# A delta-rule mixer's pair products issued ahead of its token transposes, with retention's reciprocals in halves, the slab splits and the gate's product placed beside the levels of the triangular inverse

## The chip, the cores and the metric

One core of a Trainium2 chip runs the whole program. The metric is the device time in microseconds (us) of one execution, as the median of several runs.

## The reference, cut to what matters

The program computes two blocks of a network on 512 tokens of width 1024, in float32. The change touches only the first block, whose two layers each run three mixers side by side: a delta-rule mixer of four heads of 64 (`rwkv7_mixer`), a retention mixer (`retention_mixer`) and latent attention (`mla_mixer`). Their outputs are joined and multiplied by `w_out`.

```python
def rwkv7_mixer(p, mu, w0, w2, a0, a2, g2, k_k, k_a, r_k, gn_w, gn_b, v_first, v_res):
    ...
    g = jax.nn.sigmoid(gd) @ g2
    ...
    def step(state, inp):
        rt, kt, vt, wt, kkt, at = inp
        sa = jnp.einsum('bhvk,bhk->bhv', state, -kkt)
        state = (state * wt[:, :, None, :] + sa[..., None] * (kkt * at)[:, :, None, :]
                 + vt[..., None] * kt[:, :, None, :])
        return state, jnp.einsum('bhvk,bhk->bhv', state, rt)
    ...
    bonus = jnp.sum(r_h * k_h * r_k, axis=-1, keepdims=True) * v_h
    y = (y + bonus.reshape(B, S, RW_DIM)) * g
    return y, v_first

def retention_mixer(p, positions):
    ...
    y = y * lax.rsqrt(jnp.mean(y * y, axis=-1, keepdims=True) + NORM_EPS)
    return jax.nn.silu(g) * y.reshape(B, S, RET_DIM)
```

The scan over tokens is computed in chunks of 64. Within a chunk the recurrence is a lower triangular system, and its inverse is needed.

## The kernel before, in words

Every tensor stays on the chip: `h` is the residual stream, `arena` is a pool of 53 tiles of 128x512 float32 (`A(t)` is tile t), `con` holds constants, and `banks` are the eight PSUM banks. Weights come as slabs of up to 128x2048 through a ring of two slots. A slab is split into a high and a low part for exact products of reduced-precision matmuls (L580 to L582): ScalarE casts the high part (`prepare`, L1222), VectorE subtracts it for the low part (`prepare`, L1689), and only then may SyncE load the next slab into the slot (L2466).

Each engine has its own program, written by hand, and runs it in order. TensorE's groups take the banks in turn: `group` waits until the bank's occupant of eight groups before was released by the engine that owns it, which counts up `act_released` (ScalarE) or `dve_released` (VectorE). `taken(key)` is that release, `finished(key)` is the end of the group's matmuls. `psum_ready` is counted up at the end of a group.

The place of the change is the function `rwkv(l)` on TensorE and what answers to it on ScalarE, VectorE and GpSimd (POOL). In order, in each of the two layers:

1. `retention` ends with the sums of squares "rss" (L606), whose root ScalarE takes (`deviation`, L1208). VectorE inverts it (`invert`, L1652, a reciprocal of a whole tile), multiplies it into the output (L2000) and that by the gate (L2002). The second L2002 counts up `mix_ret_ready`.
2. VectorE's `decayed` makes the scaled keys; its last instructions (L1978) free TensorE through `scan_inputs_ready`. Before that TensorE has put "bonus" into two banks, which VectorE reads at L2007.
3. TensorE transposes four tensors to token-major form, two groups each ("tok", eight groups of four transposes, L789), and ScalarE copies them out (L1385).
4. `gram` makes three sets of pair products of 64x64 blocks, "L", "N" and "M", two banks each, 32 matmuls a set (L808). ScalarE copies L (L1202). VectorE masks N and L into the first inverse Xt and X (L2020, L2022), adds the identity (L2025, L2026, the latter counting up `inverse_ready`) and masks M (L2030).
5. `low_rank(l, 2, ...)` is the gate's product "z" (two matmuls of 64x512, L606), copied by ScalarE into tiles 39 and 40 after a wait for `mix_ret_ready`, since retention's output lies there.
6. The inverse goes through five levels (block sizes 2 to 32). In a level `blocks` (L820) makes T1 for both heads of a pair, ScalarE copies T1 (L1202), then `blocks` makes Xt and X for both, each of 16 matmuls of 64x64, and VectorE adds them (L2038). GpSimd masks the next level's factor (L2431). The last level has no X. Behind levels 0 and 1 stands a group MV (`by_token`, L834).
7. `by_token` makes W and U (L834), then come the chunk products (L881), the chain of states (L930) and the outputs (L943), the two norm sums and the output projection (L580).

```python
                gram("L", "act", Af, Bf)
                gram("N", "dve", Bf, Af)
                gram("M", "dve", Kf, Af)
                low_rank(l, 2, slice(64, 128))
                last = len(LEVELS) - 1
                for n in range(len(LEVELS)):
                    for e in range(2):
                        pe.wait_ge(lower_off_ready, cnt.next(lower_off_ready))
                        if n:
                            pe.wait_ge(*taken(("Xt", l, n - 1, e)))
                        else:
                            pe.wait_ge(inverse_ready, cnt.next(inverse_ready))
                        blocks(("T1", l, n, e), "act", 19 + e, 23 + e)
```

## Time and profile before

| | us |
|---|---|
| median of 3 runs | 2264.26 |
| lowest and highest | 2262.85 and 2276.31 |
| the profiled execution | 2263.33 |
| its span, first to last instruction | 2261.5 |
| TensorE busy in the span | 2066.6 (91%) |
| VectorE busy | 1254.9 (55%) |
| ScalarE busy | 812.9 (36%) |
| GpSimd busy | 88.6 (4%) |
| mean granted TensorE clock | 0.956 of full speed |

The profile's page gives totals. A change of order in one stage is read from the timeline and the chain of waits of that stage: about 276 to 326 us in the first layer and 1019 to 1069 us in the second. A float32 matmul appears as two records, so a group of 16 matmuls of 64x64 is 32 records. A granted clock of 1.00 is 2.4 GHz and 0.50 is 1.2 GHz. Since each engine runs in order, an instruction can be late because of what stands ahead of it on its own engine, and TensorE can wait on a bank as well as on data.

### The profile page before, as it was taken

What the parts mean: (1) busy time and instruction counts of PE and PEld (TensorE: products, weight loads), DVE (VectorE), ACT (ScalarE), POOL (GpSimd) and SP (SyncE); (2) the same over time, 40 slices, a digit from 0 to 9 for tenths busy, and PEclk for the clock granted to TensorE, in tenths of its full rate; (3) what the DMA queues carried; (4) which work ended last, traced back from release to release, by engine and by line L of the source; (5) the groups of instructions that cost most, each with busy time, mean ns of one, the idle gap of its engine ahead of it and who ended that gap; (6) DMA issues with size and microseconds to landing.
All of it is one profiled execution on the core that took longest, in us unless ns stands there. A gap on an engine that the chain in (4) does not pass through costs nothing.

```text
span 2261.5 us, 29485 instructions
## 1 busy us (share of the span) xinstructions
PE 2066.6 (91%) x12698; PEld 1672.7 (74%) x12698; DVE 1254.9 (55%) x1579; ACT 812.9 (36%) x1075; POOL 88.6 (4%) x61
## 2 busy tenths in 40 slices
PE   6998688999999999868899999999999987899776
PEld 5786476888888887637688888887777666697664
DVE  8474756643444636566554334467766634563764
ACT  3244433322222324443332222246454533262522
POOL 4010020000000001012000000000000000100000
PEclk9999799999999999988999999999999989899788
DMA  5220011222322322001023233133222222121010
GB/s 196 103 77 1 1 41 38 94 96 83 112 104 77 107 101 77 1 1 40 20 93 103 80 109 108 65 122 121 77 91 92 76 75 93 33 100 64 1 38 37
DMA packets 25472, 166.81 MB, mean 74 GB/s; under 512 B 2816, under 2 KB 3072, under 8 KB 9472
## 3 DMA queue, kind: packets, MB, share of 16 engines
q1 hardware_dynamic: 25344, 164.93, 20.8%
q8 instruction: 101, 1.65, 0.3%
q14 instruction: 27, 0.22, 0.0%
HBM read 162.82 MB, written 2.10 MB: 73 GB/s over the span
## 4 chain that ended last, share of the span: by engine, by line
PE 77%; DVE 13%; ACT 7%; issue 3%; DMA 0%; DVEq 0%; SPq 0%; ACTq 0%
PE bank L580 21%; PE bank L581 21%; PE bank L582 21%; PE bank L606 4%; PE bank L820 2%; DVE ring_low L1689 2%; DVE arena L1652 2%; PE bank L727 2%; ACT ring_high L1222 1%; PE bank L714 1%; DVE arena L2171 1%; ACT arena L1481 1%; PE bank L1154 1%; DVE arena L1990 1%; PE bank L808 1%
## 5 line engine op out<-in xcount | busy, mean ns | idle before, releaser
L580 PE MATMUL bank<-arena_split,ring_high 128*128 128x512 f32 x2252 | 895.7, 398 | 63.0 <-DVE ring_low L1689 42.8
L581 PE MATMUL bank<-arena_split,ring_high 128*128 128x512 f32 x2252 | 884.2, 393 | 0.0
L582 PE MATMUL bank<-arena_split,ring_low 128*128 128x512 f32 x2252 | 883.4, 392 | 0.0
L580 PEld LDWEIGHTS bank<-arena_split,ring_high 128*128 128x128 f32 x2252 | 427.7, 190 | 167.5 <-DVE ring_low L1689 37.5
L581 PEld LDWEIGHTS bank<-arena_split,ring_high 128*128 128x128 f32 x2252 | 428.0, 190 | 92.5 <-issue 4.6
L582 PEld LDWEIGHTS bank<-arena_split,ring_low 128*128 128x128 f32 x2252 | 427.4, 190 | 90.2
L1689 DVE TENSOR_TENSOR ring_low<-ring,ring_high 128x2048 fp32r<-128x2048 f32 (+3 forms) x161 | 344.6, 2142 | 148.9 <-ACT ring_high L1222 147.9
L1222 ACT ACTIVATE ring_high<-ring 128x2048 fp32r<-128x2048 f32 (+3 forms) x161 | 284.3, 1769 | 388.5 <-PE bank L582 387.3
L1240 ACT ACTIVATE arena<-bank 128x512 f32<-128x512 f32 x72 | 43.1, 599 | 268.1 <-DVE bank L1670 268.0
L1202 ACT ACTIVATE arena<-bank 128x512 f32<-128x512 f32 (+3 forms) x113 | 58.6, 533 | 177.4 <-PE bank L582 98.0
L2118 DVE TENSOR_TENSOR arena<-arena,bank 128x512 f32<-128x512 f32 x44 | 30.3, 688 | 119.7 <-PE bank L582 118.1
L1670 DVE TENSOR_TENSOR bank<-bank,rstd 128x512 f32<-128x512 f32 x72 | 50.2, 697 | 77.5 <-PE bank L582 77.5
L1696 DVE TENSOR_TENSOR arena_split<-arena,arena_split 128x512 fp32r<-128x512 f32 x94 | 61.5, 688 | 52.8 <-ACT arena_split L1228 52.7
L1652 DVE RECIPROCAL arena<-arena 128x512 f32<-128x512 f32 x23 | 77.0, 3348 | 23.4 <-ACT arena L1208 23.3
L606 PE MATMUL bank<-arena 128*128 128x512 f32 (+8 forms) x256 | 87.6, 495 | 0.6 <-issue 0.6
L606 PE MATMUL bank<-arena,con 128*128 128x512 f32 (+1 forms) x122 | 61.6, 630 | 11.5 <-DVE arena L1645 4.3
L1228 ACT ACTIVATE arena_split<-arena 128x512 fp32r<-128x512 f32 x94 | 54.6, 622 | 28.7 <-DVE arena L2092 20.8
L580 PE MATMUL bank<-ring_high,arena_split 128*128 128x256 f32 (+1 forms) x208 | 61.4, 295 | 0.0
L582 PE MATMUL bank<-ring_high,arena_split 128*128 128x256 f32 (+1 forms) x208 | 60.5, 291 | 0.0
L581 PE MATMUL bank<-ring_low,arena_split 128*128 128x256 f32 (+1 forms) x208 | 60.5, 291 | 0.0
L1664 DVE TENSOR_TENSOR arena<-bank,rstd 128x512 f32<-128x512 f32 (+1 forms) x43 | 29.4, 688 | 53.2 <-PE bank L582 53.0
L820 PE MATMUL bank<-arena 64*64 64x64 f32 x1792 | 55.8, 221 | 3.3 <-issue 3.2
(285 smaller groups left out, 1897.3 us busy)
## 6 DMA issues: line engine op xcount, KB each, us to landing
ring<-slabs_in SPq DMA_DIRECT2D x122, 1024.0 KB, 4.8
ring<-slabs_in SPq DMA_DIRECT2D x32, 704.0 KB, 4.1
con<-con_in SPq DMA_DIRECT2D x1, 2176.0 KB, 9.7
h<-x_in SPq DMA_DIRECT2D x4, 512.0 KB, 7.4
out<-h SPq DMA_DIRECT2D x4, 512.0 KB, 2.6
ring<-slabs_in SPq DMA_DIRECT2D x3, 512.0 KB, 3.7
ring<-slabs_in SPq DMA_DIRECT2D x2, 768.0 KB, 4.3
arena<-gates_in SPq DMA_DIRECT2D x1, 1536.0 KB, 8.8
```

What stands on the lines that cost most here:

```text
L580: pe.matmul(out, weight[0], right[0], start=start, stop=False)
L581: pe.matmul(out, weight[0], right[1], start=False, stop=False)
L582: return pe.matmul(out, weight[1], right[0], start=False, stop=stop)
L606: mm = pe.matmul(b[out_rows, 0:N], w, r, start=(k == 0), stop=(k == len(weights) - 1))
L820: mm = pe.matmul(bk[rows_of(s), block(hp, j)], A(left)[at], A(right)[at], start=(hp == 0 and j == 0), stop=(hp == 1 and j == NT - 1))
L1202: f(dst, b[rows, 0:n], func, scale=scale).then_inc(cnt.up(act_released), 1)
L1222: f(ring_high[:, n % SLOTS, 0:cols], ring[:, at % SLOTS, 0:cols], ACT.Copy).then_inc(cnt.up(slab_high_ready), 1)
L1228: f(R(dst), src, ACT.Copy).then_inc(cnt.up(high_ready), 1)
L1652: dve.reciprocal(A(t)[:, 0, :], A(t)[:, 0, :]).then_inc(cnt.up(dve_done), 1)
L1670: tt(b[:, :], b[:, :], rstd[:, :], MUL).then_inc(cnt.up(scaled_ready), 1)
L1689: tt(ring_low[:, n % SLOTS, 0:cols], ring[:, at, 0:cols], ring_high[:, n % SLOTS, 0:cols].bitcast(F32), SUB).then_inc(cnt.up(slab_split), 1)
L1696: tt(R(dst), src, R(high).bitcast(F32), SUB).then_inc(cnt.up(parts_ready), 1)
```

## The change

On TensorE the three `gram` calls stand ahead of the transposes (the helper functions move with them, unchanged), and the gate's product stands behind level 3. ScalarE copies L first, then the transposes; it casts the two slabs of the output projection one behind level 2 and one behind the last level, and copies z behind level 3's T1. VectorE no longer inverts and multiplies retention's factor ahead of the bonus: it does the bonus, multiplies retention's sum by its gate, and works off the rest between the additions of the levels, the reciprocal in four halves of 256 columns. No other stage is touched. GpSimd's and SyncE's programs are the same.

```diff
 # TensorE
                 pe.wait_ge(scan_inputs_ready, cnt.next(scan_inputs_ready))
...
+                gram("L", "act", Af, Bf)
+                gram("N", "dve", Bf, Af)
+                gram("M", "dve", Kf, Af)
                 pe.wait_ge(values_ready, cnt.next(values_ready))
                 for n, src in enumerate((14, 33, 35, 27)):
...
-                gram("L", "act", Af, Bf)
-                gram("N", "dve", Bf, Af)
-                gram("M", "dve", Kf, Af)
-                low_rank(l, 2, slice(64, 128))
                 last = len(LEVELS) - 1
                 for n in range(len(LEVELS)):
...
+                    if n == last - 1:
+                        low_rank(l, 2, slice(64, 128))
 # ScalarE
                 for hp in range(2):
                     deviation(("rss", l, hp), A(hp)[:, 0, :], 64)
-                prepare(f"out{l}_0")
-
+                for e in range(2):
+                    copy_out(("L", l, e), A(17 + e)[:, 0, :])
                 for n in range(4):
...
-                for e in range(2):
-                    copy_out(("L", l, e), A(17 + e)[:, 0, :])
-
-                act.wait_ge(mix_ret_ready, cnt.next(mix_ret_ready))
-                for i in range(2):
-                    copy_out(("z", l, 2, i), A(39 + i)[:, 0, :])
                 for n in range(len(LEVELS)):
                     for e in range(2):
                         copy_out(("T1", l, n, e), A(49 + e)[:, 0, :])
                     if n < 2:
                         copy_out(("MV", l, n), A(35 + n)[:, 0, :])
+                    if n == 2:
+                        prepare(f"out{l}_0", 1)
+                    if n == len(LEVELS) - 2:
+                        act.wait_ge(mix_ret_ready, cnt.next(mix_ret_ready))
+                        for i in range(2):
+                            copy_out(("z", l, 2, i), A(39 + i)[:, 0, :])
+                prepare(f"out{l}_0")
 # VectorE
                 decayed()
-                for hp in range(2):
-                    invert(("rss", l, hp), hp)
-                    y = A(39 + hp)[:, 0, :]
-                    tt(y, y, A(hp)[:, 0, :], MUL).then_inc(cnt.up(dve_done), 1)
-                    dve.wait_ge(cnt.sem, cnt.value)
-                    tt(A(2 + hp)[:, 0, :], y, A(23 + hp)[:, 0, :], MUL).then_inc(cnt.up(mix_ret_ready if hp else dve_done), 1)
                 dve.wait_ge(values_ready, cnt.next(values_ready))
                 for hp in range(2):
                     dve.wait_ge(psum_ready, finished(("bonus", l, hp)))
                     b = bank(("bonus", l, hp))
                     tt(A(37 + hp)[:, 0, :], b[:, :], v_(hp), MUL).then_inc(cnt.up(dve_released), 1)
-                prepare(f"out{l}_0")
+                for hp in range(2):
+                    dve.wait_ge(*taken(("ry", l, hp)))
+                    tt(A(39 + hp)[:, 0, :], A(39 + hp)[:, 0, :], A(23 + hp)[:, 0, :], MUL).then_inc(cnt.up(dve_done), 1)
+                dve.wait_ge(cnt.sem, cnt.value)
+
+                def retention_factor(hp, half):
+
+                    dve.wait_ge(*taken(("rss", l, hp)))
+                    r = A(hp)[:, 0, half * (T // 2):(half + 1) * (T // 2)]
+                    dve.reciprocal(r, r).then_inc(cnt.up(dve_done), 1)
+
+                def retention_output(hp):
+
+                    dve.wait_ge(cnt.sem, cnt.value)
+                    tt(A(2 + hp)[:, 0, :], A(39 + hp)[:, 0, :], A(hp)[:, 0, :], MUL).then_inc(cnt.up(mix_ret_ready if hp else dve_done), 1)
+
+                beside = {(0, 0): lambda: retention_factor(0, 0), (0, 1): lambda: retention_factor(0, 1),
+                          (1, 0): lambda: retention_factor(1, 0), (1, 1): lambda: retention_factor(1, 1),
+                          (2, 0): lambda: retention_output(0), (2, 1): lambda: retention_output(1),
+                          (3, 0): lambda: prepare(f"out{l}_0", 1)}
...
                             tt(M[:, e, :], M[:, e, :], b[:, :], ADD).then_inc(cnt.up(dve_released), 1)
+                        if (n, e) in beside:
+                            beside[n, e]()
+                prepare(f"out{l}_0")
                 state = flat(14, 3)
```

TensorE's order around the inverse in the kernel before, from retention's sums of squares (L606 with `con`) to the last level. L789 are the transposes, L808 the three grams, L606 with `small` the gate's product, L820 the levels' blocks, L834 MV, then W and U.

```order
L606 MATMUL bank<-arena,con 128x512 x4
L789 MATMUL bank<-con,arena 128x128 x32
L808 MATMUL bank<-arena 64x64 x96
L606 MATMUL bank<-arena,small 128x512 x2
L820 MATMUL bank<-arena 64x64 x96
L834 MATMUL bank<-arena 64x64 x16
...
L820 MATMUL bank<-arena 64x64 x256
L834 MATMUL bank<-arena 64x64 x64
```

The same stretch in the changed kernel, where the grams are L798, the transposes L838, the levels' blocks L810 and MV, W and U L824.

```order
L606 MATMUL bank<-arena,con 128x512 x4
L798 MATMUL bank<-arena 64x64 x96
L838 MATMUL bank<-con,arena 128x128 x32
L810 MATMUL bank<-arena 64x64 x96
L824 MATMUL bank<-arena 64x64 x16
...
L810 MATMUL bank<-arena 64x64 x192
L606 MATMUL bank<-arena,small 128x512 x2
L810 MATMUL bank<-arena 64x64 x64
L824 MATMUL bank<-arena 64x64 x64
```

The grams and the transposes change places, and the gate's product goes from ahead of level 0 to between levels 3 and 4.

VectorE's order in the kernel before, from the last instructions of `decayed` (L1978) to the additions of the levels (L2038).

```order
L1978 TENSOR_TENSOR arena<-arena,decay_end 128x512 x2
L1652 RECIPROCAL arena<-arena 128x512
L2000 TENSOR_TENSOR arena<-arena 128x512
L2002 TENSOR_TENSOR arena<-arena 128x512
L1652 RECIPROCAL arena<-arena 128x512
...
L2007 TENSOR_TENSOR arena<-bank,arena 128x512 x2
L1689 TENSOR_TENSOR ring_low<-ring,ring_high 128x2048 x2
L2020 TENSOR_TENSOR arena<-bank,con 128x512
...
L2030 TENSOR_TENSOR arena<-bank,con 128x512 x2
L2038 TENSOR_TENSOR arena<-arena,bank 128x512 x18
```

The same stretch in the changed kernel, where L1980 ends `decayed`, L2003 is the bonus, L2006 the product with the gate, L2013 a half reciprocal, L2018 retention's output, L1691 a slab's low part and L2053 the levels' additions.

```order
L1980 TENSOR_TENSOR arena<-arena,decay_end 128x512 x2
L2003 TENSOR_TENSOR arena<-bank,arena 128x512 x2
L2006 TENSOR_TENSOR arena<-arena 128x512 x2
L2035 TENSOR_TENSOR arena<-bank,con 128x512
...
L2045 TENSOR_TENSOR arena<-bank,con 128x512 x2
L2053 TENSOR_TENSOR arena<-arena,bank 128x512 x2
L2013 RECIPROCAL arena<-arena 128x256
...
L2018 TENSOR_TENSOR arena<-arena 128x512
...
L1691 TENSOR_TENSOR ring_low<-ring,ring_high 128x2048
L2053 TENSOR_TENSOR arena<-arena,bank 128x512 x4
L1691 TENSOR_TENSOR ring_low<-ring,ring_high 128x2048
```

The bonus stands directly behind `decayed`, nothing long stands between it and the masks, and the reciprocals and slab splits are spread among the additions.

## Rows read from the trace of the kernel before

**Rows 1.** The page, engines' busy us, share of the span and instructions.
```profile
PE 2066.6 (91%) x12698; PEld 1672.7 (74%) x12698; DVE 1254.9 (55%) x1579; ACT 812.9 (36%) x1075; POOL 88.6 (4%) x61
```

**Rows 2.** Chain of waits, first layer, 276 to 326 us: start, length, engine, tile, line.
```profile
276.05 3.27 DVE arena L1652
...
285.39 0.69 DVE arena L2007
286.22 1.94 PE bank L789 x8
288.16 4.72 PE bank L808 x192
292.88 1.91 PE bank L606 x4
294.79 1.46 issue
296.25 1.15 PE bank L820 x32
...
303.97 5.60 PE bank L820 x192
309.57 0.93 PE bank L834 x32
```

**Rows 3.** Timeline, first layer: start, length, engine, line, tiles, count, idle before and releaser.
```profile
271.36 3.70 ACT L1222 ACTIVATE ring_high<-ring 128x2048 fp32r<-128x2048 f32 x2
...
276.10 5.38 PE L789 MATMUL bank<-con,arena 128*128 128x128 f32 x24 [3.65 <-DVE arena L1978]
...
291.85 0.69 DVE L2020 TENSOR_TENSOR arena<-bank,con 128x512 f32<-128x512 f32 x1 [0.78 <-PE bank L808]
292.46 1.16 DVE L2022 TENSOR_TENSOR arena<-arena,con 128x512 f32<-128x512 f32 x1
...
297.27 1.28 DVE L2030 TENSOR_TENSOR arena<-bank,con 128x512 f32<-128x512 f32 x2
...
302.82 1.15 PE L834 MATMUL bank<-arena 64*64 64x64 f32 x32
...
353.55 0.80 PE L580 MATMUL bank<-arena_split,ring_high 128*128 128x512 f32 x1
```

**Rows 4.** Timeline, second layer, the same columns.
```profile
1018.95 4.51 PE L789 MATMUL bank<-con,arena 128*128 128x128 f32 x24 [3.65 <-DVE arena L1978]
...
1029.06 1.94 PE L789 MATMUL bank<-con,arena 128*128 128x128 f32 x8 [5.61 <-DVE arena L2007]
...
1038.35 7.62 PE L820 MATMUL bank<-arena 64*64 64x64 f32 x192 [1.29 <-issue]
...
1045.78 1.11 PE L834 MATMUL bank<-arena 64*64 64x64 f32 x32
...
1099.17 0.79 PE L580 MATMUL bank<-arena_split,ring_high 128*128 128x512 f32 x1
```

**Rows 5.** Groups of instructions, 276 to 330 us: busy us, mean ns, idle before.
```profile
L2038 DVE TENSOR_TENSOR arena<-arena,bank 128x512 f32<-128x512 f32 x18 | 12.4, 689 | 15.3 <-PE bank L820 15.3
L2431 POOL TENSOR_TENSOR arena<-arena,con 128x512 f32<-128x512 f32 x10 | 10.8, 1094 | 33.6 <-PE bank L820 17.5 <-ACT arena L1202 16.0
L1202 ACT ACTIVATE arena<-bank 128x512 f32<-128x512 f32 x16 | 9.5, 598 | 26.0 <-PE bank L820 12.8 <-PE bank L834 8.8 <-PE bank L606 3.0
L1652 DVE RECIPROCAL arena<-arena 128x512 f32<-128x512 f32 x2 | 6.7, 3342 | 0.0
L1689 DVE TENSOR_TENSOR ring_low<-ring,ring_high 128x2048 fp32r<-128x2048 f32 x2 | 4.5, 2282 | 0.0
```

**Rows 6.** Busy time in stretches: PE, PEld, DVE, ACT, POOL (records), PEclk, DMA share, GB/s.
```profile
278.00:280.00 2.00, 2.00 (x12) 2.00 (x11) 1.97 (x2) 1.38 (x3) 0.00 (x0) 0.50 0.00 0
...
290.00:292.00 2.00, 2.00 (x86) 2.00 (x81) 1.22 (x2) 1.09 (x2) 1.11 (x2) 0.50 0.88 328
298.00:300.00 2.00, 2.00 (x76) 2.00 (x73) 0.98 (x2) 0.65 (x2) 1.67 (x2) 1.00 0.04 8
1022.00:1024.00 2.00, 1.45 (x11) 1.21 (x9) 1.93 (x4) 1.74 (x4) 0.00 (x0) 0.88 0.00 0
1040.00:1042.00 2.00, 2.00 (x43) 2.00 (x42) 0.65 (x2) 0.57 (x2) 1.06 (x2) 0.50 0.00 0
```

20 lines of the change are left out of this document (10 added, 10 removed).

## The prediction, made before the changed kernel was run

> **What bounds the kernel now.** I read the page first, then the chain of waits in the two stretches that the diff touches, then the timeline there, the groups of instructions, and last the busy time with the clock. The page says that TensorE is busy for 2066.6 of 2261.5 us [rows 1], so what can be won lies in TensorE's waits and in its slow stretches, and both are in stages like this one.
>
> The chain of the first layer shows the stage. TensorE starts its transposes at 276.10, when VectorE has finished `decayed` (L1978), does 24 of 32 (six groups) in 5.38 us [rows 3], and then stops. The seventh group takes the bank of the first "bonus", and VectorE releases that bank only at L2007, at 285.39, because two whole reciprocals and four products stand ahead of it [rows 2]. The last two groups run from 286.22. Grams follow for 4.72 us and the gate's product for 1.91, then comes a gap of 1.46 in which TensorE waits for `inverse_ready`, and level 0 starts at 296.25 [rows 2]. VectorE has to mask and add eight times before it gives that signal, and again its queue sets it: it begins with L2020 at 291.85 and is at M (L2030) at 297.27 [rows 3]. From `scan_inputs_ready` to the first T1 the first layer thus takes 296.25 - 276.10 = 20.15 us. In the second layer it is 1038.35 - 1018.95 = 19.40 us, with a wait of 5.61 on the same L2007 and a gap of 1.29 before level 0 [rows 4].
>
> Within the levels TensorE is the bound. A level without MV is six groups, 192 records, in 5.60 us, and MV adds 0.93 [rows 2], with no idle time in it. VectorE's four additions of 0.69 fill less than half of that; over the stretch they come with 15.3 us of waiting for TensorE [rows 5]. Level 0 alone is slow: from its start to MV it takes 302.82 - 296.25 = 6.57 us in the first layer [rows 2, 3] and 1045.78 - 1038.35 = 7.43 in the second [rows 4], since the second T1 waits for the second `inverse_ready`, and in the second layer also because the granted clock is 0.50 from 1040 to 1042 [rows 6].
>
> **The grams first.** At 276.10 the grams start. At that point TensorE has idled for 3.65 us [rows 3] and the clock is at 0.50 [rows 6], so I take their length from the first layer, where the clock was at 0.50 too (290 to 292 [rows 6]): 4.72 us [rows 2]. Then eight groups of transposes. At 0.50 one group is 4 x 5.38 / 24 = 0.90 us [rows 3]; in the row with the clock at 0.88, 11 took 1.45 us, so a group is 0.53 [rows 6]. The grams need two banks each and the transposes the same eight, so: transposes 1 and 2 wait for the bonus, which VectorE now reads right after `decayed`, by about +1.3 us; 3 and 4 for L, copied by ScalarE; 5 and 6 for N; 7 and 8 for M. VectorE can mask N from 291.85 - 288.16 = 3.7 us after the start of the grams and has released the second M bank at 297.27 + 1.28 - 288.16 = 10.4 us after it [rows 2, 3]. What VectorE does between (two bonus products, two with the gate, 0.69 each [rows 5]) ends at +2.8, before N is there, and costs nothing. The eighth transpose group therefore starts no earlier than +10.4 and ends at +10.9 to +11.3; TensorE's own work alone would end at 4.72 + 8 x 0.53 = 9.0 to 4.72 + 8 x 0.90 = 11.9. I take +11.2 for the first T1, the bank bound with the last group at a middle length. `inverse_ready` is given before M and so is no wait any more. The gain is 20.15 - 11.2 = 8.95 us in the first layer and 19.40 - 11.2 = 8.2 in the second.
>
> **Level 0 without its wait.** It should take the six groups' 5.60: gains of 6.57 - 5.60 = 0.97 and 7.43 - 5.60 = 1.83.
>
> **The gate's product.** It costs 1.91 us [rows 2] and goes from ahead of level 0 to between levels 3 and 4, where TensorE has no gap: minus 1.91 in each layer. It is no loss against before, only the part of the 20.15 that is paid elsewhere.
>
> **VectorE's work beside the levels.** The half reciprocal has no row. A whole one is 3.34 [rows 5]; half of that is 1.67 if time goes by columns, and 3.34 if it did not. I take 1.67, since the products beside it do go by columns in the same profile (0.69 for 512, 2.28 for 2048 [rows 5]). Count from the end of Xt of the first head: X is added by +1.7, the half reciprocal ends at +3.4, the second Xt is added at +4.1, and T1 of the second head in the next level wants that at 5 x 0.93 = +4.7 with MV between. It fits with 0.6 to spare. X is added at +4.7 and the second half ends at +6.4, while TensorE's next Xt ends at +6.5. Levels 1 and 2 go alike, and retention's products (0.69) are short. In level 3 the slab's low part of 2.28 stands between: Xt of the second head is added at 1.7 + 2.28 + 0.7 = +4.6 counted as above (the end of the first Xt), and T1 of the second head wants it at 4 x 0.93 + 1.91 = +5.6, because the gate's product stands in between. Cover 1.0; without that product the wait would be 0.9. The last slab's low part falls into W and U (four groups, 3.7 us) with nothing behind it that is wanted sooner. Cost of all of it: 0, with bounds of 0 and, by the longer reciprocal, of 4 x 3.34 + 8 x 0.69 = 18.9 us on VectorE in levels 0 and 1, against 2 x (5.60 + 0.93) = 13.1 us of TensorE: 5.8 us a layer, 11.6 in all.
>
> **ScalarE and SyncE.** Two casts of 1.85 (3.70 for the pair [rows 3]) move into ScalarE's idle time, which is 26.0 us around its 16 copies [rows 5]; the one behind level 2 ends before T1 of level 3 is there. GpSimd has the same ten masks of 1.09 [rows 5], each wanted four groups after its release. The next slabs are fetched some 20 us later than now, and the output projection, which starts at 353.55 [rows 3], works on the two already split. Nothing.
>
> The Trainium skill speaks against one edit. Its page "SBUF — State Buffer", section "Who interferes with whom", says that a VectorE instruction with both inputs in SBUF competes with a GpSimd instruction that reads SBUF, one holding off the other for a whole instruction. The trace agrees in size: L2022 took 1.16 us, beside a mask on GpSimd, where its like takes 0.69 [rows 3, 5]. By that rule the slab's low part could start up to 1.09 later, which would use up the cover of 1.0; the sum would be worse by 0.1 a layer.
>
> **The sum.** 8.95 + 8.2 + 0.97 + 1.83 - 2 x 1.91 = 16.1 us. The profiled execution took 2263.33, so it would take 2247.2. It lies 0.93 under the median of 2264.26, so the median should be 2248.2.
>
> **Rivals.**
> A, VectorE's work does not fit between the additions: the half reciprocal is nearer to a whole one or the additions slip. For it speaks the slack of only 0.6 us, against it the 15.3 us of idle time [rows 5]. At the full 5.8 a layer the gain is 16.1 - 11.6 = 4.5 and the time 2259.8; at half of that, 2254.
>
> B, the clock stays at 0.50 through all transposes: T1 starts at +11.9, and one low stretch of 2 us as in 1040 to 1042, where 43 records started in place of 76 [rows 6], costs 0.9 more. That is 1.6 a layer, gain 12.9, time 2251.4.
>
> C, the clock gives back more. From MV to the projection the first layer takes 353.55 - 302.82 = 50.7 us, the second 1099.17 - 1045.78 = 53.4 [rows 3, 4]. Should the shift in time let the second layer keep its clock, 2.7 more are won: 2245.5. It can as well go the other way in the first.
>
> D, slower than before: the levels run at 1.2 GHz. They have 960 records a layer. At 2.0 / 43 against 2.0 / 76 us each [rows 6] a record costs 20.2 ns more, 19.4 us a layer and 38.8 in all: 16.1 less that is a loss of 22.7, and the time 2287.0. It decides from 16.1 / 0.0202 = 797 records at low clock, some 37 us. For it speaks that the second layer's clock fell although TensorE was nearly always busy; against it that it was 1.00 with TensorE fully busy at 298 [rows 6], and that the gaps go away. The Trainium skill's page "TensorE: Matmul & The Clock Gate", section "A second HAM failure mode: psum-queue depth-cycling", has a kernel whose small gaps between groups that cycle through the banks kept its clock switching; that is this rival, and only 1040 to 1042 bears it out here.
>
> E, the change does not do what it says: TensorE is held by the next thing, the masks of M, for much longer. Were only the gap of 4.7 to 5.6 won, the time would be 2254; the work that leaves VectorE's queue ahead of the masks, two reciprocals and two slab parts, 11.2 us [rows 5], speaks against it.
>
> **How the numbers follow.** The forecast, with a range of its own from 2244.5 to 2252, gets 0.62; A 0.13; B 0.09; C 0.08; E 0.05; D 0.03. The range of 8 in 10 goes from 2243.5 to 2256: it takes in B, C and E, half of A, and leaves out D and the far end of A. A measurement of this kernel can tell about 1%, 22.6 us, from no change. All but D and a far tail of C lie within it: faster by over 1% 0.04, within 1% 0.93, slower by over 1% 0.03.
>
> **What would show it.** Right: the first T1 about 11 us after `decayed` in both layers, no wait of TensorE on the bonus, level 0 in 5.6 us, half reciprocals of 1.7 us, the gate's product between levels 3 and 4 with no wait behind it, and everything from W on the same, only about 8 us earlier a layer. Wrong: waits of TensorE for L2053 in levels 0 to 4, a half reciprocal over 2.3 us, the clock at 0.50 inside the levels, or a T1 later than +12.

## The result and the profile after

The changed kernel takes 2251.44 us (median of 20 runs, 2244.39 to 2266.94) beside 2263.56 for the kernel before in the same comparison (20 runs, 2257.71 to 2276.31). The ratio is 0.9943 with a 95% interval of 0.9928 to 0.9959, a gain of about 13 us (9 to 16). The profiled execution took 2248.42 us with a span of 2246.6, against 2263.33 and 2261.5. The forecast was 2248.2 with a range from 2243.5 to 2256. The first row of the page answers to [rows 1]; TensorE's busy time fell by 11.2 us although its instructions are the same in number.

```profile
PE 2055.4 (91%) x12698; PEld 1662.6 (74%) x12698; DVE 1253.7 (56%) x1583; ACT 811.8 (36%) x1075; POOL 91.3 (4%) x61
```

In what follows a layer is cut at three marks: the end of VectorE's `decayed`, where TensorE begins again after 3.65 us of idling; the first T1 of level 0; and the first instruction of W. The time from the first to the third is called the stage. All of the change lies in it, but for the last slab split and the fetches of the next slabs, which now fall behind W. The marks are starts of rows of TensorE's timeline, as in [rows 3] and [rows 4].

| us | before, layer 1 | after, layer 1 | before, layer 2 | after, layer 2 |
|---|---|---|---|---|
| start to first T1 | 20.15 | 10.50 | 19.40 | 11.69 |
| first T1 to MV | 6.57 | 6.32 | 7.43 | 6.47 |
| MV to W | 23.51 | 25.57 | 23.64 | 25.68 |
| stage | 50.23 | 42.39 | 50.47 | 43.84 |
| W to the output projection | 27.22 | 29.14 | 29.75 | 29.86 |

The stage gives 7.84 + 6.63 = 14.5 us. What is left of the difference of the spans comes from parts in which TensorE's order has no edit: W to the projection is 1.9 + 0.1 longer, the stretch between the layers 2.2 longer (667.63 for 665.40), what lies ahead of the first stage 0.3 shorter, and all behind the second projection 4.4 shorter (1157.93 for 1162.33). The sum is 14.9. These outer parts jump from kernel to kernel, some of them between a few values, as the experiments show, so only the stage is evidence for a cause.

TensorE's timeline of the changed kernel in the first layer, with start, length, engine, line, tiles, count, and idle time before with its releaser:

```profile
275.81 3.03 PE L798 MATMUL bank<-arena 64*64 64x64 f32 x192 [3.65 <-DVE arena L1980]
278.77 2.84 PE L838 MATMUL bank<-con,arena 128*128 128x128 f32 x24
284.44 1.94 PE L838 MATMUL bank<-con,arena 128*128 128x128 f32 x8 [2.83 <-DVE arena L2045]
286.31 6.48 PE L810 MATMUL bank<-arena 64*64 64x64 f32 x192
292.63 1.10 PE L824 MATMUL bank<-arena 64*64 64x64 f32 x32
...
318.20 3.95 PE L824 MATMUL bank<-arena 64*64 64x64 f32 x128 [0.91 <-DVE arena L2053]
```

The same view in the second layer:

```profile
1014.97 4.50 PE L798 MATMUL bank<-arena 64*64 64x64 f32 x192 [3.65 <-DVE arena L1980]
...
1024.93 1.80 PE L838 MATMUL bank<-con,arena 128*128 128x128 f32 x8 [2.13 <-DVE arena L2045]
1026.66 6.64 PE L810 MATMUL bank<-arena 64*64 64x64 f32 x192
```

The wait on the bonus (4.74 and 5.61 before) and the wait ahead of level 0 (1.46 and 1.29) are gone. There is one in their place, again on a bank: the last two groups of transposes take M's two banks, and TensorE stands for 2.83 and 2.13 us until VectorE's mask L2045 has read them. (In the second layer there is also a stop of 0.55 us ahead of the first transposes, whose row names no releaser.) VectorE's timeline shows why it comes when it comes:

```profile
278.19 0.69 DVE L2035 TENSOR_TENSOR arena<-bank,con 128x512 f32<-128x512 f32 x1
...
283.61 1.28 DVE L2045 TENSOR_TENSOR arena<-bank,con 128x512 f32<-128x512 f32 x2
290.04 0.69 DVE L2053 TENSOR_TENSOR arena<-arena,bank 128x512 f32<-128x512 f32 x1 [5.15 <-PE bank L810]
...
291.58 1.75 DVE L2013 RECIPROCAL arena<-arena 128x256 f32<-128x256 f32 x1
```

From the first mask of N (L2035) to the end of M's (L2045) VectorE works for 6.7 us without a gap. Then it idles for 5.15, which is to say that its work is short enough but stands in an order that leaves M for last. The chain that ended last (start, length, what) gives the lengths without overlap, of level 0 in its first row and of level 1 in its last:

```profile
286.38 6.41 PE bank L810 x192
...
293.72 5.60 PE bank L810 x192
```

The busy time of stretches, with the columns of [rows 6], shows the clock on both sides of the new wait:

```profile
276.00:278.00 2.00, 2.00 (x148) 2.00 (x147) 2.00 (x4) 0.96 (x2) 0.22 (x1) 1.00 0.03 8
...
286.00:288.00 2.00, 2.00 (x36) 1.69 (x36) 0.00 (x0) 0.76 (x2) 0.00 (x0) 0.55 0.04 8
...
1016.00:1018.00 2.00, 2.00 (x84) 2.00 (x83) 1.31 (x3) 0.98 (x2) 0.24 (x1) 0.50 0.03 8
...
1026.00:1028.00 2.00, 2.00 (x29) 1.67 (x28) 0.00 (x0) 1.11 (x2) 0.00 (x0) 0.50 0.04 8
```

In the first layer the grams found the clock at 1.00 (3.03 us), in the second mostly at 0.50 (4.50). In both layers level 0 begins at 0.50 to 0.55, that is mostly at the lower of the two levels, 1.2 GHz, right behind the wait on M. Its six groups take 6.41 in place of 5.60.

### The profile page after: what moved, and what is told of

It is laid out like the page before. It is cut to its first block, busy times and chain, and to the rows that moved or that the text cites. A ratio compares the mean times of both kernels' runs of the same rounds, so it can differ in the third digit from the quotient of the medians.

```text
span 2246.6 us, 29491 instructions
## 1 busy us (share of the span) xinstructions
PE 2055.4 (91%) x12698; PEld 1662.6 (74%) x12698; DVE 1253.7 (56%) x1583; ACT 811.8 (36%) x1075; POOL 91.3 (4%) x61
## 4 chain that ended last, share of the span: by engine, by line
PE 76%; DVE 13%; ACT 7%; issue 3%; DMA 0%; DVEq 0%; SPq 0%; ACTq 0%
PE bank L580 21%; PE bank L581 21%; PE bank L582 21%; PE bank L606 4%; PE bank L810 2%; DVE ring_low L1691 2%; PE bank L727 2%; ACT ring_high L1223 1%; DVE arena L1654 1%; PE bank L714 1%; DVE arena L2189 1%; ACT arena L1483 1%; DVE arena L1992 1%; PE bank L824 1%; ACT arena L1339 0%
## 5 line engine op out<-in xcount | busy, mean ns | idle before, releaser
L1691 DVE TENSOR_TENSOR ring_low<-ring,ring_high 128x2048 fp32r<-128x2048 f32 (+3 forms) x161 | 345.3, 2145 | 149.6 <-ACT ring_high L1223 148.7
L606 PE MATMUL bank<-arena 128*128 128x512 f32 (+8 forms) x256 | 87.9, 496 | 0.6 <-issue 0.6
L1654 DVE RECIPROCAL arena<-arena 128x512 f32<-128x512 f32 x19 | 63.6, 3350 | 23.6 <-ACT arena L1209 23.5
L606 PE MATMUL bank<-arena,con 128*128 128x512 f32 (+1 forms) x122 | 62.3, 637 | 11.5 <-DVE arena L1647 4.3
L810 PEld LDWEIGHTS bank<-arena 64*64 64x64 f32 x1792 | 54.5, 138 | 2.3 <-issue 2.2
```

Source lines behind the costliest of these rows:

```text
L606: mm = pe.matmul(b[out_rows, 0:N], w, r, start=(k == 0), stop=(k == len(weights) - 1))
L810: mm = pe.matmul(bk[rows_of(s), block(hp, j)], A(left)[at], A(right)[at], start=(hp == 0 and j == 0), stop=(hp == 1 and j == NT - 1))
L1654: dve.reciprocal(A(t)[:, 0, :], A(t)[:, 0, :]).then_inc(cnt.up(dve_done), 1)
L1691: tt(ring_low[:, n % SLOTS, 0:cols], ring[:, at, 0:cols], ring_high[:, n % SLOTS, 0:cols].bitcast(F32), SUB).then_inc(cnt.up(slab_split), 1)
```

## Experiments

Each kernel was timed against the kernel before. The stage is given as layer 1 / layer 2, from one profiled execution each. The first five runs take the change apart, the others go after the new wait and the old one ahead of W.

**The changed kernel a second time.** No edit. It was run in one comparison with M's masks first, the gate's product last, and both together, as their reference.

> The changed kernel again, unaltered, as the yardstick for the kernels beside it and for how much varies outside of the stage. All theories: stage from decayed's end to W 42.4 to 43.9 us a layer, gain against before 9 to 16 us.

Measured: 2247.99 us (6 runs, 2243.63 to 2254.82), ratio 0.9910 (0.9886 to 0.9935). Stage 42.35 / 43.69, first T1 at +10.50 / +11.64. The stage repeats within 0.2 us, the median moves by 3.5. A difference of a few us between medians of this kernel in different comparisons is therefore no evidence.

**VectorE's new order without the grams' new place.** The changed kernel, with the transposes (and ScalarE's copies of them) back ahead of the grams. The gate's product and ScalarE's casts stay where the change put them, so this run shows VectorE's order together with these.

```diff
-                gram("L", "act", Af, Bf)
-                gram("N", "dve", Bf, Af)
-                gram("M", "dve", Kf, Af)
...
                         mm.then_inc(psum_ready, 1)
+                gram("L", "act", Af, Bf)
+                gram("N", "dve", Bf, Af)
+                gram("M", "dve", Kf, Af)
...
+                        pe.wait_ge(*taken(("M", l, 1)))
```

> The changed kernel with TensorE's transposes put back ahead of the grams (ScalarE's copies likewise). Theory (two waits: the bonus' bank and inverse_ready; VectorE's new order removes the first, the grams' early place the second): transposes start with decayed's end and no longer stop, eight groups in about 6.6 us, N is there at +9, and the first T1 at +13.3 us against +10.5 and +11.7 in the changed kernel; stage from decayed's end to W about 45.8 us a layer (changed kernel 42.4 and 43.8, before 50.2 and 50.5), so a gain of about 9 us against before, 5 less than the changed kernel. Rival 1 (all of the gain is VectorE's lighter queue): stage as in the changed kernel, 42.4 to 43.8, gain 14. Rival 2 (all is TensorE's order): stage as before, 50, no gain.

Measured: stage 44.42 / 44.76, first T1 at +11.85 / +11.76; 2261.44 us (10 runs, 2244.60 to 2269.69), ratio 0.9963 (0.9931 to 0.9994). TensorE's timeline:

```profile
272.37 5.38 PE L835 MATMUL bank<-con,arena 128*128 128x128 f32 x32 [3.66 <-DVE arena L1981]
...
284.22 7.17 PE L810 MATMUL bank<-arena 64*64 64x64 f32 x192 [3.51 <-issue]
```

All 32 transposes go through in one piece: with the bonus read directly behind `decayed`, no bank is held. Then TensorE waits 3.51 us ahead of level 0. The row names no releaser; by the order of the program it is for VectorE's masks. Of the 14.5 us in the stage, VectorE's order brings 5.8 + 5.7 = 11.5, with the gate's product already paid behind level 3. The grams' place brings the other 2.0 + 0.9, because the masks then run beside the transposes. Both figures come from one profiled execution; the whole only bounds them, since the ratio stands for a gain of 8 us with an interval from 1 to 16. The theory had expected a stage of 45.8 and the first T1 at +13.3, so it came 1.0 to 1.4 us better than that.

**TensorE's new order alone.** The kernel before, with the grams ahead of the transposes; VectorE keeps reciprocals and slab splits ahead of bonus and masks.

```diff
                         gram("M", "dve", Kf, Af)
+                pe.wait_ge(values_ready, cnt.next(values_ready))
+                for n, src in enumerate((14, 33, 35, 27)):
...
+                            mm = pe.transpose(b[:, j * P:(j + 1) * P], A(src + hp)[:, 0, j * P:(j + 1) * P],
+                                              cst("ident"))
```

> The kernel before with only the grams ahead of the transposes (and L copied first); VectorE keeps reciprocals, products and both slab splits ahead of its masks. Theory: the first transposes stop on the bonus' bank until +9.3 us, the last on M's bank until about +22, the gate's product follows, the first T1 at about +24 us; stage from decayed's end to W about 54 us a layer, 4 more than before: 8 us slower than before, about 2271. Rival 1 (only VectorE's queue counts): as before. Rival 2 (TensorE's order is the gain): stage 43, gain of 14.

Measured: stage 58.42 / 58.00, 8.2 and 7.5 us longer than before, first T1 at +27.08 / +27.63; 2281.31 us (10 runs), ratio 1.0060 (1.0038 to 1.0082). It is slower, by about 14 us, and the stage grew by nearly twice the 4 us a layer of the theory. TensorE's timeline:

```profile
272.64 4.38 PE L798 MATMUL bank<-arena 64*64 64x64 f32 x192 [3.66 <-DVE arena L1978]
283.61 3.65 PE L838 MATMUL bank<-con,arena 128*128 128x128 f32 x16 [6.58 <-DVE arena L2008]
...
294.14 1.94 PE L838 MATMUL bank<-con,arena 128*128 128x128 f32 x8 [3.17 <-DVE arena L2031]
296.01 3.78 PE L606 MATMUL bank<-arena,small 64*128 64x512 f32 x4
```

The grams take the first six banks, so now the very first transposes wait for the bonus (L2008), and the last two for M (L2031), which stands behind two slab splits. The last transposes come at +21.5 us, as expected, but then take 1.94 us, and the gate's product takes 3.78, not the 1.91 of [rows 2]. Level 0 begins at 0.50, as the busy time of its first 4 us shows:

```profile
300.00:304.00 4.00, 4.00 (x80) 4.00 (x80) 0.00 (x0) 1.58 (x3) 1.60 (x2) 0.50 0.00 0
```

So the parts don't add. The grams' place alone costs 15.7 us in the stages, and on top of VectorE's order it wins 3.0.

**The bonus alone.** The kernel before, with the bonus moved ahead of retention's reciprocals, and nothing else.

```diff
+                dve.wait_ge(values_ready, cnt.next(values_ready))
+                for hp in range(2):
+                    dve.wait_ge(psum_ready, finished(("bonus", l, hp)))
+                    b = bank(("bonus", l, hp))
+                    tt(A(37 + hp)[:, 0, :], b[:, :], v_(hp), MUL).then_inc(cnt.up(dve_released), 1)
                 for hp in range(2):
                     invert(("rss", l, hp), hp)
...
```

> The kernel before with one edit: VectorE reads the bonus' banks ahead of retention's reciprocals. Theory (two waits in series on one queue): TensorE's stop of 4.7 and 5.6 us on the bonus' bank goes, but VectorE reaches the masks of N only at about +15.1 us as before (two reciprocals, four products and two slab splits stand ahead), so the first T1 comes at +19.4 us against 20.15 and 19.40; stage 49.5 to 50 us, gain under 1 us a layer. Rival (each wait counts by itself): stage 45 to 46 us, gain 10.

Measured: stage 50.91 / 50.43, first T1 at +19.05 / +19.04; 2268.34 us (10 runs), ratio 1.0006 (0.9986 to 1.0026). The wait of 4.7 to 5.6 us is gone, but nothing is gained by it. TensorE's timeline:

```profile
272.65 5.38 PE L789 MATMUL bank<-con,arena 128*128 128x128 f32 x32 [3.65 <-DVE arena L1978]
...
291.70 8.51 PE L820 MATMUL bank<-arena 64*64 64x64 f32 x190 [8.79 <-issue]
```

Its length comes back in one piece ahead of level 0, 8.79 us. VectorE still has its whole queue ahead of the masks, and `inverse_ready` comes when that queue is done, whoever waited where before. What limits the start of the levels is the sum of VectorE's work ahead of the masks, not the wait that the chain of before showed first.

**Whole reciprocals beside the levels.** The changed kernel, with the two halves of each reciprocal put together again behind the first X of levels 0 and 1.

```diff
-                beside = {(0, 0): lambda: retention_factor(0, 0), (0, 1): lambda: retention_factor(0, 1),
-                          (1, 0): lambda: retention_factor(1, 0), (1, 1): lambda: retention_factor(1, 1),
+                beside = {(0, 0): lambda: retention_factor(0), (1, 0): lambda: retention_factor(1),
```

> The changed kernel with each reciprocal whole (512 columns) behind the first head's additions of levels 0 and 1, none behind the second's. Theory (the halves are needed): the second head's Xt is added 1.0 us too late, T1 of the second head waits 1.0 us in levels 1 and 2 of each layer, 2 us a layer, 4 us in all: gain against before 4 us smaller than the changed kernel's. Rival (there is room anyway): no wait of TensorE on the additions, stage as in the changed kernel.

Measured: stage 44.74 / 46.01, 2.4 / 2.2 longer than the changed kernel; 2256.13 us (10 runs), ratio 0.9959 (0.9929 to 0.9990). VectorE's timeline and, under it, TensorE's:

```profile
292.33 3.35 DVE L2013 RECIPROCAL arena<-arena 128x512 f32<-128x512 f32 x1
```

```profile
294.31 1.10 PE L810 MATMUL bank<-arena 64*64 64x64 f32 x32
296.32 5.02 PE L810 MATMUL bank<-arena 64*64 64x64 f32 x159 [0.91 <-issue]
...
304.24 5.95 PE L810 MATMUL bank<-arena 64*64 64x64 f32 x197 [0.97 <-issue]
```

The addition of the second head's Xt comes 1.6 us later than with a half, and T1 of that head, which had 0.6 us of slack by the forecast, waits 0.91 and 0.97. The halves are needed; the releaser of these waits is not named in the row, but the place of the first, behind 32 records of the level, is the one that the forecast's count gives.

**M's gram behind the transposes.** The changed kernel, with only the third gram moved back behind the transposes, so that M's banks are no longer between them.

```diff
                 gram("N", "dve", Bf, Af)
-                gram("M", "dve", Kf, Af)
...
                         mm.then_inc(psum_ready, 1)
+                gram("M", "dve", Kf, Af)
...
+                        pe.wait_ge(*taken(("M", l, 1)))
```

> The changed kernel with the gram M moved behind the transposes (and a wait for its masks ahead of MV). Theory (what is left is the wait for M's bank, 2.8 and 2.1 us, and the fall of the clock behind it): that wait goes, the first T1 comes at +8 to +10 us, with the clock at 1.00; stage 39.5 to 41.5 us a layer, 2 to 3 less than the changed kernel, gain against before 19 to 20 us (about 2244). Rival (TensorE's own work or inverse_ready is as late): the first T1 at +10.5 to +11.7, stage as in the changed kernel.

Measured: first T1 at +8.22 / +8.13, level 0 in 5.60 / 5.87, stage 39.62 / 40.19; 2241.44 us (7 runs, 2234.07 to 2250.40), ratio 0.9907 (0.9875 to 0.9939). TensorE's timeline:

```profile
272.19 2.67 PE L798 MATMUL bank<-arena 64*64 64x64 f32 x128 [3.65 <-DVE arena L1981]
274.79 4.71 PE L837 MATMUL bank<-con,arena 128*128 128x128 f32 x32
279.43 1.16 PE L798 MATMUL bank<-arena 64*64 64x64 f32 x64
280.41 5.78 PE L810 MATMUL bank<-arena 64*64 64x64 f32 x192
```

From `decayed` to MV no wait is left. M's masks run beside level 0, where VectorE idled in the changed kernel, and MV, their first reader, comes 5.6 us later.

A second time, in another comparison:

> The kernel with M behind the transposes again, beside the one before it in this list. All theories: stage 39.6 to 40.2 us. If the gate's product behind level 4 is worth its 0.9 us a layer, this one is 1.8 us slower than the kernel beside it.

Measured: first T1 at +8.12 / +8.10, level 0 in 6.12 / 5.89, stage 40.94 / 39.55; 2241.51 us (6 runs, 2236.84 to 2252.48), ratio 0.9894 (0.9866 to 0.9922). The medians of the two comparisons are 0.1 us apart. Against the changed kernel (2251.44 and 2247.99) it is 6 to 10 us less, and the stages account for 6.4 us the first time and 5.6 us the second, against the changed kernel's own second profile. It has the lowest medians of this study; its interval still touches that of the changed kernel's second comparison (0.9886 to 0.9935). The 6.12 us of level 0 came with the granted clock at 1.00 throughout, so level 0 can lose 0.5 us in this kernel without a fall of the clock.

**M's masks first.** Another way to the same end: VectorE masks M before it adds the identity four times.

```diff
-                dve.wait_ge(cnt.sem, cnt.value)
-                for e in range(2):
-                    tt(eight(X[:, e, :]), eight(X[:, e, :]), own("ident_heads"), ADD).then_inc(cnt.up(dve_done), 1)
...
                 for e in range(2):
                     dve.wait_ge(psum_ready, finished(("M", l, 1)))
...
+                dve.wait_ge(cnt.sem, cnt.value)
+                for e in range(2):
+                    tt(eight(X[:, e, :]), eight(X[:, e, :]), own("ident_heads"), ADD).then_inc(cnt.up(dve_done), 1)
...
```

> The changed kernel with VectorE's two masks of M ahead of the four identity additions; TensorE's order as in the changed kernel. Theory (the transposes wait for M's bank, which VectorE's queue sets): M's banks come free 2.7 us earlier, at about +6.7 us, TensorE's wait goes, inverse_ready comes 1.3 us later and then sets the first T1 at about +8.4 us and the second about 0.3 after its turn; stage 40.0 to 41 us a layer, 2 to 3 less than the changed kernel. Rival (the wait goes over whole to inverse_ready or TensorE's own work is the bound): first T1 at +10 or later, stage as in the changed kernel.

Measured: first T1 at +8.71 / +8.99, stage 41.90 / 40.49; 2249.26 us (6 runs), ratio 0.9913 (0.9888 to 0.9939). TensorE's timeline:

```profile
281.47 4.41 PE L810 MATMUL bank<-arena 64*64 64x64 f32 x134 [0.53 <-issue]
286.51 1.90 PE L810 MATMUL bank<-arena 64*64 64x64 f32 x58 [0.63 <-issue]
```

The wait on M is gone here too, and small ones of 0.5 to 0.7 us stand in its place. They have no releaser in the rows; that they are for the identity additions, which now come later, is read from the order of the program. In the first layer level 0 took 6.73 us, and the stage missed the 40 to 41 us of the theory by 0.9. The cause of the wait on M is the order of VectorE's queue, then. Of the two cures the one that leaves VectorE alone has the shorter stages (by 0.3 to 2.3 us a layer in its two profiled executions) and the lower medians (2241.4 and 2241.5).

**The gate's product last.** The changed kernel, with the gate's product between level 4 and W, and both slab splits behind the levels, to take the wait of 0.91 us ahead of W.

```diff
-                    if n == last - 1:
+                    if n == last:
...
-                          (2, 0): lambda: retention_output(0), (2, 1): lambda: retention_output(1),
-                          (3, 0): lambda: prepare(f"out{l}_0", 1)}
+                          (2, 0): lambda: retention_output(0), (2, 1): lambda: retention_output(1)}
```

> The changed kernel with the gate's product behind level 4 in place of level 3 and both slab splits of VectorE behind the levels (ScalarE's casts behind levels 2 and 3). Theory (W waits 0.9 us in each layer for the last addition, and the product of 1.9 us can cover that): no wait ahead of W, stage 41.5 and 42.9 us, 0.9 less a layer than the changed kernel; VectorE's two splits end in time for G. Rival (the split behind the levels, or ScalarE's copies of z, make W's copies or G late): the 0.9 comes back between W and the chunk products, same time.

Measured: stage 40.51 / 42.56, so 1.9 and 1.3 less, but W to the projection 30.25 / 31.32, so 1.1 and 1.5 more; 2253.77 us (12 runs), ratio 0.9940 (0.9920 to 0.9960). The wait ahead of W is gone, and MV to W is 1.2 and 1.3 us shorter. There is no gain in the whole. The other 0.7 us of the first layer lie in level 0, which took 5.65 although TensorE waited for M as before:

```profile
281.83 1.16 PE L838 MATMUL bank<-con,arena 128*128 128x128 f32 x8 [2.02 <-DVE arena L2044]
282.92 5.82 PE L810 MATMUL bank<-arena 64*64 64x64 f32 x192
```

The granted clock was 1.00 through this wait and level 0, where the changed kernel's level 0 began at 0.55. In the kernel with whole reciprocals it was the same in the first layer: a wait of 1.74 us, transposes in 1.16, level 0 in 5.65. In both of them the grams had been slow (4.58 and 5.40 us, mostly at 0.50), while in the changed kernel's first layer they ran in 3.03.

What came back behind W is a gap of TensorE with no releaser, within the chunk products and the grams behind W. It is there in the kernel before and in the changed one also, and shorter. The rows are TensorE's timeline, one fence for each kernel; first before, then the changed kernel, then this one:

```profile
335.59 0.93 PE L808 MATMUL bank<-arena 64*64 64x64 f32 x49 [1.37 <-issue]
...
1077.29 0.75 PE L881 MATMUL bank<-arena 64*64 64x64 f32 x23 [0.80 <-issue]
```

```profile
327.18 0.93 PE L798 MATMUL bank<-arena 64*64 64x64 f32 x49 [1.09 <-issue]
...
1067.43 0.75 PE L882 MATMUL bank<-arena 64*64 64x64 f32 x23 [1.54 <-issue]
```

```profile
323.34 0.93 PE L798 MATMUL bank<-arena 64*64 64x64 f32 x49 [2.46 <-issue]
...
1063.40 0.75 PE L882 MATMUL bank<-arena 64*64 64x64 f32 x23 [3.00 <-issue]
```

**Both.** M's gram behind the transposes and the gate's product last, that is the edits of the two kernels together.

> The gram M behind the transposes and the gate's product behind level 4 with both slab splits behind the levels, together. Theory (two separate waits, 2 to 3.7 us and 0.9 us a layer): stage 38.7 and 39.3 us, gain against before 21 to 24 us, about 2242; it beats the changed kernel by 7 to 9 us. Rival (the parts share a gain): no better than with M behind the transposes alone (39.6 and 40.2).

Measured: stage 39.17 / 38.97, shorter than any before it; W to the projection 29.48 / 34.61; 2247.54 us (6 runs), ratio 0.9909 (0.9884 to 0.9933). The stage is what the theory said, the time is not: 2242 was expected. The gaps are there again (2.27 and 3.10 us). In the second layer the fetch of the two next slabs, which SyncE starts when the splits have released their ring places, runs up to the gap and ends within it. The first fence is the timeline, the second the busy time of a stretch ahead of the gap and of one behind it, with the DMA share as the last column but one:

```profile
1052.22 2.53 SPq L2484 DMA_DIRECT2D ring<-slabs_in  x2
...
1061.22 0.75 PE L883 MATMUL bank<-arena 64*64 64x64 f32 x23 [3.10 <-issue]
```

```profile
1054.00:1057.00 3.00, 2.30 (x116) 2.17 (x116) 0.45 (x2) 1.19 (x2) 0.00 (x0) 1.00 0.98 396
...
1078.00:1081.00 3.00, 1.78 (x17) 1.10 (x15) 1.45 (x3) 1.08 (x2) 0.00 (x0) 0.50 0.00 0
```

The last row is further behind the gap: the clock is at 0.50 there. Of the 4.8 us that W to the projection is longer than in the changed kernel, the gap is 1.6. The rest is not the gap's: the second run of M behind the transposes, with a gap of only 1.51, took 33.93 for the same part, with the clock at 0.50 in places as well.

**The same with the fetches earlier.** As the last kernel, but the slab splits stand beside levels 2 and 3, so that the first fetch of each layer starts 8 to 9 us earlier.

```diff
-                          (2, 0): lambda: retention_output(0), (2, 1): lambda: retention_output(1)}
+                          (2, 0): lambda: retention_output(0), (2, 1): output_and_slab,
+                          (3, 1): lambda: prepare(f"out{l}_0")}
```

> As the kernel with M late and the gate's product behind level 4, but VectorE's slab splits behind the second head's additions of levels 2 and 3, so that the two 1024 KB slabs are fetched some 9 and 4 us earlier. Theory (in the kernel with late splits TensorE's gaps without a releaser in the chunk products and the RB gram, 2.3 us in the first layer and 3.1 in the second against 1.4 and 0.8 before, come from the slabs' fetches running at the same time): stage 38.7 to 39.3 as there, gaps back to 0.8 to 1.5 us, W to the projection 27 and 30 us against 29.5 and 34.6 there, time 3 to 6 us under it. Rival (the gaps come with the gate's product's new place): gaps and W to the projection as there.

Measured: stage 39.27 / 38.64; W to the projection 28.75 / 31.28; 2246.74 us (6 runs), ratio 0.9912 (0.9887 to 0.9937). The 3 to 6 us under the last kernel that the theory expected in the whole did not come (0.8). The gaps fell to 0.69 and 1.00 us:

```profile
323.34 0.93 PE L798 MATMUL bank<-arena 64*64 64x64 f32 x49 [0.69 <-issue]
...
1057.78 0.75 PE L883 MATMUL bank<-arena 64*64 64x64 f32 x23 [1.00 <-issue]
```

The same TensorE order, with the fetches ended about 5 us ahead of the gap, loses 1.6 and 2.1 us less in it. That speaks strongly for the slab fetches, though the edit moved VectorE's splits along with them; in the last kernel these splits had ended 3.7 us or more before the gap began. The fetches only make the gaps longer: in the kernel before no slab is fetched in the 7 us ahead of them, and they are 1.37 and 0.80. What TensorE waits for in them is not shown. The page lists a queue named "instruction" of 101 packets on the same DMA engines, and an instruction fetch held up by the slabs would fit; no run here tested it. And the kernel as a whole is not faster than the one with only M's gram moved (2246.74 beside 2241.51 in the same comparison), though the gate's product in its new place was expected to make it 1.8 us faster. Its part behind the second projection took 1168.8 us in the profiled execution, against 1157.9, and no edit reaches there.

## Why the prediction was right, and where it was not

**What bounds the stage: right, and tested.** The prediction held that VectorE's queue sets both the bank wait and the start of level 0. The bonus alone bought nothing in the stage, VectorE's order 11.5 us. Taking away only the wait that the chain names first was worth nothing. One reading in it is off, without touching the sum: VectorE gives the first `inverse_ready` after four masks and two additions, not after eight instructions; in the kernel before, the sixth ends as level 0 starts, and the last two only concern the second head.

**Start to first T1: 8.95 + 8.2 forecast, 9.65 + 7.71 measured.** The bank bound was named as the next limit, and it is what TensorE waits for. The two misses have opposite signs, and two sources. The forecast took the grams at the low clock in both layers. In the second layer they ran so (4.50 us for 4.72) and M's second bank came free at +10.4, as worked out. In the first the clock was at 1.00, the grams took 3.03 us, N was ready at +2.4 and not +3.7, and all behind it came 1.3 us earlier. The last transposes were slower than assumed: the last two groups took 1.94 and 1.80 us, nearly all of it at the price of the low clock, where the sum had one group of middle length behind the bank.

**Level 0: 0.97 + 1.83 forecast, 0.25 + 0.96 measured.** This is the term that was mis-sized. "It should take the six groups' 5.60" counted the end of the wait for `inverse_ready` but not a fall of the clock. Behind the new wait on M the granted clock is 0.50 to 0.55, and level 0 takes 6.32 and 6.47. The forecast had named the clock at 0.50 inside the levels as a sign of being wrong, and here it came. With the wait on M taken away by moving its gram, level 0 took 5.60 in the first layer of three profiled executions and 6.12 in that of a fourth, and 5.75 to 5.89 in the second layer. So most of the missing 1.6 us is the low clock behind the new wait: about 0.7 in the first layer and 0.6 in the second; the remaining 0.3 of the second layer stays without that wait as well. But the wait alone does not decide it: with the gate's product last and with whole reciprocals the first layer had a wait of 2.02 and 1.74 us, kept the clock at 1.00 and did level 0 in 5.65. What decides it stays open. Rival B had this term, a low stretch of 0.9 us a layer, but with low transposes throughout, and the first 24 of them ran in 2.84 and 2.78 us, under 0.5 a group.

**The gate's product: 1.91 a layer forecast, 2.06 and 2.04 measured** for MV to W as a whole. No more than 0.15 us a layer is left for anything else, so VectorE's work beside the levels cost next to nothing, as forecast.

**The half reciprocal: 1.67 forecast, 1.75 measured.** It goes by columns but for 0.08 us. The slack of 0.6 us that the count gave is borne out by the whole reciprocals, which are 1.6 us longer and made TensorE wait 0.9 to 1.0. Rival A is thereby right as a mechanism and wrong in this kernel.

**The slab split's hold-off: right in kind, larger than priced.** The timeline of the changed kernel shows it beside GpSimd's L2458, in the first layer and then in the second:

```profile
309.40 4.12 POOL L2458 TENSOR_TENSOR arena<-con,decay_end 128x512 f32<-128x512 f32 x2
...
310.32 2.29 DVE L1691 TENSOR_TENSOR ring_low<-ring,ring_high 128x2048 fp32r<-128x2048 f32 x1
...
1049.91 2.08 POOL L2458 TENSOR_TENSOR arena<-con,decay_end 128x512 f32<-128x512 f32 x2
...
1050.97 3.17 DVE L1691 TENSOR_TENSOR ring_low<-ring,ring_high 128x2048 fp32r<-128x2048 f32 x1
```

In the first layer GpSimd was held off (4.12 us for two that take 2.08 in the second), in the second VectorE (3.17 for 2.29). The Trainium skill's "SBUF — State Buffer", section "Who interferes with whom", says that such a pair contends for a port that is locked by one of them, and that the order of issue decides who blocks. The trace agrees: either was the one that waited, and by about the length of the other's instruction (0.9 us beside a product of 1.04, 2.0 beside the split of 2.29). T1 of the second head was not late in either layer; the gate's product (1.98 us) stands between.

**From W on: "the same" was only half right.** In the first layer W to the projection took 1.9 us more. The busy time of the last 15 us ahead of the projection shows TensorE's clock at 0.77, where it was 1.00 in the kernel before. The first fence is before, the second after:

```profile
338.00:353.00 15.00, 9.64 (x294) 7.14 (x295) 9.84 (x24) 2.46 (x5) 0.00 (x0) 1.00 0.01 3
```

```profile
332.00:347.00 15.00, 11.16 (x285) 8.89 (x280) 7.96 (x18) 2.35 (x4) 0.00 (x0) 0.77 0.02 3
```

Rival C held that a shift in time could change the clock here, in either direction. In the first layer it lost. In the second the clock did what the rival said: it was 0.78 from 1084 to 1099 us in the kernel before and 1.00 from W to the projection after, and TensorE was busy for 2.2 us less there (19.76 for 21.95). The part still took as long (29.75 before, 29.86 after), because stops without a releaser took the gain away: the one above grew from 0.80 to 1.54, and a new one of 1.35 appeared.

```profile
1080.41 0.34 PE L913 MATMUL bank<-arena 64*64 64x64 f32 x6 [1.35 <-issue]
```

**The sum.** 16.1 us forecast for the stages, 14.5 measured: 0.2 more up to T1, 1.6 less in level 0, 0.3 less for the gate's product. The profiled time came out 1.2 us from the forecast 2247.2 because parts outside the stage gave 0.4 on balance. That closeness is partly luck, since those parts moved by +1.9, +0.1, +2.2, -0.3 and -4.4 to get there. The forecast of the median, 2248.2, was off by 3.2, since the profiled execution lies 3.0 under the median of its kernel and not 0.9. The medians of the two comparisons, 2251.44 and 2247.99, show how much of this is chance. They also show that the time can't tell the forecast from rival B, whose 2251.4 is the first of them to 0.1 us; only the rows of the stage can, and they have the forecast right up to T1 and the rival nearer in level 0.

**What stays open.** Why the parts that no edit touches take one of a few values: what lies ahead of the first stage 272.2 to 272.8 or 275.5 to 276.7 us, all behind the second projection 1157.8 to 1158.7, 1162.3 to 1162.6 or 1168.8 to 1169.3, over all kernels run. The last of these alone makes a difference of 11 us, more than most edits here. The traces say where it lies: not in the first 900 us behind the second projection, where TensorE's busy time agrees within 1.1 us over all kernels, but in what follows. That took 257.9 us at a mean granted clock of 0.90 in the changed kernel and 269.2 at 0.87 with M's masks first, with TensorE busy for 208.0 and 219.4. So it goes with the clock; why the clock differs there was not tested.

## What to carry to other kernels

Where an engine cycles through a fixed number of banks, the reader who frees a bank late stops the writer n groups on; list who owns the bank of each group, and put the group whose reader is last behind those that need nothing of that reader. A wait in the chain is worth its length only if the same queue does not set a later one: here the wait of 5 us alone was worth nothing, and taking the work away ahead of the masks was worth 11.5. When work is put beside TensorE's, cut it to the slack between two additions (1.7 us fitted, 3.3 did not), and judge by the touched stage, since the whole also carries shifts of the clock elsewhere.

## What the runs showed of the hardware that was not expected

- A wait of 2 to 3 us can have a second price. TensorE idled 2.83 and 2.13 us for M's bank, and level 0 behind it began at a granted clock of 0.55 and 0.50, which cost it 0.6 to 0.7 us. It need not: behind waits of 2.02 and 1.74 us in two other kernels the clock stayed at 1.00. In the kernel with the grams' place alone the gate's product behind a chain of longer waits took 3.78 us, where it takes 1.98 otherwise.
- TensorE stops within long runs of small matmuls without a releaser. The stops behind W took 0.7 to 1.8 us where no slab or one slab was fetched in the 7 us ahead, and 2.3 to 3.1 us where two were fetched one behind the other up to the stop, at a DMA share of 0.98.
- VectorE and GpSimd hold each other off in either direction: 3.17 us for a split of 2.29, and 4.12 for two GpSimd products of 2.08.
